# A two-block network on one NeuronCore: the SBUF tensors laid out at other start addresses

## The reference

```python
def first_block(x, ...):            # one layer
    mod = silu(c) @ ada_w + ada_b   # nine modulation vectors
    h = h + 0.5 * g1 * rmsnorm(swiglu(y, ...))        # 1024 -> 2816 -> 1024
    h = h + g2 * rmsnorm(token_mix(y, ...))           # mLSTM heads and HGRN2 heads, w_in, w_out
    h = h + 0.5 * g3 * rmsnorm(swiglu(y, ...))

def second_block(x, ...):           # two layers
    m = neighborhood_attention(...) or diff_attention(...)
    x = x + rms_norm(m, g[1])
    f = conv_glu_ffn(rms_norm(x, g[2]), ...)          # 1024 -> 2 * 2816 -> 1024
    x = x + rms_norm(f, g[3])
    x = x + sigmoid(rms_norm(x, g[4]) @ ple_w_gate) * (p @ ple_w_proj)
```

## The kernel before

| tensor | begins at | past 512 |
|---|---|---|
| h | 16512 | 128 |
| yh, yl, ph, pl | 32896, 49280, 53376, 57472 | 128 |
| raw, wh, wl | 65664, 82048, 98432 | 128 |
| acc, cst | 127232, 131328 | 256 |
| hidh, hidl | 139008, 184064 | 256 |
| oh, ol, gh, gl, moh, mol | 139008 to 188160 | 256 |
| PT, dv, qkh | 179968, 171776, 211712 | 256 |

## Time and profile before

### The profile page before, as it was taken

How to read it: one execution, slowest core, us unless ns; L and a number is a source line. 1 busy time by engine, 2 the same in 40 slices (tenths; PEclk the granted TensorE clock), 3 DMA queues, 4 the chain that set the end, 5 groups by cost and what they waited for, 6 DMA issues and landing times.

```text
span 2619.6 us, 29183 instructions
## 1 busy us (share of the span) xinstructions
PE 2494.6 (95%) x11538; PEld 1977.7 (75%) x11538; DVE 1523.7 (58%) x2379; ACT 1008.7 (39%) x1547; POOL 154.3 (6%) x166
## 2 busy tenths in 40 slices
PE   7999998989987999998999999999999999999998
PEld 4878876867766888886877688887777767888876
DVE  5876436677647333336654855534866668555445
ACT  4222234444545322223444433333545554333333
POOL 0000111000010000010101000001100010000100
PEclk9999999999999999999999999999999999999999
DMA  9555427422212333222321222222232212222321
GB/s 365 170 193 193 143 89 157 105 53 54 60 42 67 111 98 98 93 89 73 99 79 57 95 98 97 93 97 93 81 102 70 79 39 91 97 97 93 104 86 65
DMA packets 233704, 265.90 MB, mean 102 GB/s; under 512 B 8376, under 2 KB 222008, under 8 KB 233568
## 3 DMA queue, kind: packets, MB, share of 16 engines
q1 hardware_dynamic: 220704, 223.39, 28.1%
q0 software_dynamic: 11088, 37.46, 4.4%
q10 hardware_dynamic: 1776, 3.18, 0.3%
HBM read 259.78 MB, written 10.75 MB: 103 GB/s over the span
## 4 chain that ended last, share of the span: by engine, by line
PE 62%; DVE 6%; issue 3%; ACT 3%; POOL 0%; DMA 0%; POOLq 0%; ACTq 0%; DVEq 0%
PE G L2044 54%; DVE wl L1343 1%; PE X L2044 1%; PE G L2499 1%; PE X L2479 1%; ACT yh L820 1%; DVE yl L1369 1%; DVE h L1432 1%; PE G L2437 1%; DVE tmpA L1384 1%; PE X L2404 1%; PE X L2488 1%; ACT wh L771 1%; PE X L2418 0%; DVE nbias L1821 0%
## 5 line engine op out<-in xcount | busy, mean ns | idle before, releaser
L1343 DVE TENSOR_TENSOR wl<-raw,wh 128x1024 fp32r<-128x1024 f32 (+1 forms) x398 | 474.8, 1199 | 695.3 <-ACT wh L771 695.0
L2044 PE MATMUL G<-yh,wh 128*128 128x512 f32 x1864 | 754.2, 405 | 49.9 <-DVE yl L1361 15.7
L2044 PE MATMUL G<-yl,wh 128*128 128x512 f32 x1864 | 732.7, 393 | 0.0
L2044 PE MATMUL G<-yh,wl 128*128 128x512 f32 x1864 | 732.3, 393 | 0.0
L771 ACT ACTIVATE wh<-raw 128x1024 fp32r<-128x1024 f32 (+1 forms) x398 | 410.0, 1037 | 821.0 <-PE G L2044 803.0
L2044 PEld LDWEIGHTS G<-yh,wh 128*128 128x128 f32 x1864 | 353.9, 190 | 150.1 <-issue 31.5
L2044 PEld LDWEIGHTS G<-yl,wh 128*128 128x128 f32 x1864 | 353.5, 190 | 76.1
L2044 PEld LDWEIGHTS G<-yh,wl 128*128 128x128 f32 x1864 | 354.0, 190 | 71.6 <-issue 2.4
L2044 PE MATMUL G<-hidh,wh 128*128 128x512 f32 x704 | 279.7, 397 | 0.0
L2044 PE MATMUL G<-hidl,wh 128*128 128x512 f32 x704 | 278.0, 395 | 0.0
L2044 PE MATMUL G<-hidh,wl 128*128 128x512 f32 x704 | 278.0, 395 | 0.0
(11 more groups left out here) (351 smaller groups left out, 3001.3 us busy)
## 6 DMA issues: line engine op xcount, KB each, us to landing
raw<-in_ffn_w_in SPq DMA_DIRECT2D x44, 1024.0 KB, 5.0
raw<-in_ffn_w_gate SPq DMA_DIRECT2D x22, 1024.0 KB, 5.4
raw<-in_ffn_w_up SPq DMA_DIRECT2D x22, 1024.0 KB, 5.3
ada_c<-in_ada_w POOLq DMA_DIRECT2D x20, 1024.0 KB, 5.6
raw<-in_ffn_w_down SPq DMA_DIRECT2D x16, 1024.0 KB, 5.1
raw<-in_w_in SPq DMA_DIRECT2D x16, 1024.0 KB, 9.5
raw<-in_ffn_w_out SPq DMA_DIRECT2D x16, 1024.0 KB, 5.3
ada_z<-in_ada_w SPq DMA_DIRECT2D x14, 1024.0 KB, 10.9
```

The costliest lines, as they stand in the source:

```text
L1343: nc.vector.tensor_tensor(place(wl), src, f32(place(wh)), ALU.subtract).then_inc(lo, 1)
L2044: ins = nc.tensor.matmul(bank, a, b, start=first and i == 0, stop=last and i == 2)
```

## The change

It reorders the `sb(...)` calls and lays five small tensors into unused columns of others. No instruction is added, removed or moved: on every engine the instructions stand in the same order before and after, with the same shapes; only names of small tensors differ (`silc` is a part of `sm`, `t5` of `lamc`, `small` of `mod`, `rcol` of `lbc`).

```diff
+        cst = sb("cst", [P, 320])
+        sm = sb("sm", [P, 32])
         h = sb("h", [P, KT, S])
 ...
         yl = sb("yl", [P, KT, S], F32R)
+        coef = sb("coef", [P, 6, KT])
+        lbc = sb("lbc", [P, 4, NH])
         raw = sb("raw", [P, 2, UNIT])
         wh = sb("wh", [P, 4, KT, P], F32R)
         wl = sb("wl", [P, 4, KT, P], F32R)
         A2 = sb("tmpA", [P, 2, S])
+        acc = sb("acc", [P, S])
+        R = sb("rstd", [P, S])
+        ms = sb("ms", [P, S])
         with ExitStack() as c:
             ada_c = sb("ada_c", [P, UNIT], F32, c)[:, :]
+        C2 = sb("tmpC", [P, 2, S])
         B2 = sb("tmpB", [P, 2, S + 16])
-        C2 = sb("tmpC", [P, 2, S])
-        acc = sb("acc", [P, S])
-        R = sb("rstd", [P, S])
-        cst = sb("cst", [P, 320])
 ...
         ones = sb("ones", [P, P])
-        ms = sb("ms", [P, S])
         vec = sb("vec", [P, 448])
-        small = sb("small", [64, 16])
         mod = sb("mod", [P, 80])
-        coef = sb("coef", [P, 6, KT])
-        lbc = sb("lbc", [P, 4, NH])
-        sm = sb("sm", [P, 32])
+        small = mod[0:64, 72:80]
         lamc = sb("lamc", [P, 16])
-        t5 = sb("t5", [32, 16])
-        silc = sb("silc", [P, 16])
-        rcol = sb("rcol", [P, 16])
+        t5 = lamc[0:32, 8:16]
+        silc = sm[:, 24:32]
+        rcol = lbc[:, 3, :]
```

## The result

The changed kernel takes 2604.74 us (median of 4 runs, 2601.19 to 2609.38) against 2623.36 us before: a ratio of 0.9934, 95% interval 0.992 to 0.9949. It is faster by 18.6 us, clear of the scatter but under 1%, where I had forecast 91. The profiled execution is the slowest of the four, 2609.38 us, with a span of 2607.6.

What follows compares the result with a forecast made beforehand. The prediction took the distance between PE's matmul starts as the bound; gains of 38.9 + 33.6 + 18.6 = 91 us gave 2532 us, likeliest case 2485 to 2560, 8 in 10 within 2485 to 2630.

Steps and rivals of the forecast that it cites:

- What bounds the kernel: Whole kernel: it is as long as its matmuls, set by the distance between two matmul starts on PE.
- The excess depends on layout: All full-rate matmuls: the 13.3 to 20.1 ns over 213.3 depend on start addresses and need not be there.
- the feed-forwards' first half: 4224 matmuls with `yh`/`yl` moving go from 226.7 to 217.5 ns, fully on the path: 38.9 us gained.
- the second half: Feed-forwards, 2112 matmuls with `hid` moving go from 233.4 to 217.5 ns, fully on the path: 33.6 us gained.
- the rest: Stretches where PE sometimes waits, 1368 and 960 matmuls: 26.5 us, of which 0.7 counted, 18.6 us gained.
- The lower bound: New distance per matmul at best, from the plain float32 stream: 213.3 + 1.3 = 214.6 ns.
- the first rival: Only `hid`, `oh` and the like gain; all stand at 226.7 ns, a fixed price per weight load; about 2611 us, chance 0.15.
- the likeliest case: All matmuls with moving activations: the excess mostly goes, to about 217.5 ns each; 2532 us, chance 0.55.
- The rival "nothing": `yh` and `hid` differ for some reason other than addresses; the time stays at 2623 us, chance 0.12.
- The slower rival: Excess grows with the distance between moving and stationary starts: 240 ns at 256 apart, +96 us, 2719 us, chance 0.18.
- Weights as moving operand: 1152 matmuls with weights moving: taken as 0, between ends of +7.7 us and -13.8 us.
- The factor 0.7: Share of the gain outside the dense stretches that reaches the time, as PE waits there; from 0.4 to 1.

Runs made afterwards that it cites:

- two tables: Two kernels of matmuls alone, with moving or stationary tensors placed at many starts: 227.1 to 233.3 ns per matmul in one, 226.7 to 234.2 in the other.
- the finer streams: Kernel of matmuls alone, weights moved in steps from 16 bytes, then other shapes: 226.7 ns at 0 and 16 bytes apart, 233.1 at 32.

## Why the prediction was wrong, step by step

**What bounds the kernel: right.** PE's matmul starts set the time in the dense stretches, and the time followed them there in each of the layouts.

**The excess depends on layout: half right.** Between 226.7 and 233.4 ns it does. The 13.3 ns below do not. The step that failed is in the change part by part: "From above, for the case that the excess mostly goes, I take half of today's smaller one, 220 ns. I take about the middle, 217.5 ns." It rests on "neither needs to be there". Measured: 226.4 to 227.0 ns in the streams of 512 columns after, and no pair of starts in two tables under 226.7. The term for the feed-forwards' first half, 38.9 us, was therefore 0; that for the second half, 33.6 us, was 2112 x 6.7 = 14.2; of that for the rest, 18.6 us, at most 5.4 could be there. The lower bound was taken from a plain float32 stream at half the rate, and no row showed a stream at full rate near it; the lowest fp32r stream of 512 separate columns in the runs has 226.7. What I had in hand and set too low was the first rival's argument, the equal 13.3 ns with 512 and 256 columns, a fixed price that does not care for shape. The time measured lies inside my range for 8 in 10, 2485 to 2630 us, but by this rival, to which I had given 0.15, and outside the likeliest case's own range, 2485 to 2560: that is luck and not a confirmation.

**The first rival: right in its distances, wrong in its reason.** It said 226.7 for all and 2611 us; measured are about 226.5 and 2604.7, since the 4 to 8 us that it charged for the moving weights were not lost. It is not the start at 256 that was bad but the 128 bytes between it and the weights: moved to a multiple of 512 alone, `hid` kept 233.2 ns, and at 128 with the weights at 128 it had 226.9.

**The rival "nothing": refuted.** `hid` fell by 6.9 ns, and the time by 18.6 and 16.1 us in two measurements.

**The slower rival: right in its reason, wrong in its size.** The distance between the operands counts, but with a period of 256 bytes. I had two points of that curve, 0 and 128, and drew a line through them to 240 ns at 256. The layout with the weights at 128 is the slower case that can really be reached, 232.3 ns and a ratio of 1.0075.

**Weights as moving operand: the value 0 was right, by luck.** 120.0 ns before and after. I had taken 0 as lying between two ends, and neither end came. The lower one, 108 ns "if the distance between the two counts", was wrongly derived: their distance to the stationary activation was already 0 and went to 256. That 0 and 256 are the same place on the curve would explain 120.0 ns, but at 128 apart these products took 118.2, so they do not seem to follow the curve at all; why is open.

**The factor 0.7 stays open.** Of 18.6 us gained, 14.2 are `hid` in the dense stretches, which leaves 4.4 of 960 x 5.6 = 5.4 us for the rest. In the layout with the weights at 128 nearly nothing of the mixed stretches reached the time. In the traces themselves, the four stretches with `hid` moving, from their first start to their last, take 501.6 us before and 488.3 after, 13.3 less; everything else up to the end of the last matmul takes 2112.8 us before and 2114.1, 2111.6, 2111.3 and 2110.2 in the four layouts at 0 or 256 apart. So of the 5.4 us between -1.3 and 2.6 showed, which speaks for less than 0.7, but one profile of each, scattering by 4 us, can't fix the factor.

**The Trainium skill's 215.8 ns** (TensorE: Matmul & The Clock Gate, Back-to-back issue gap) agrees with the plain bf16 streams, 215.8 ns, and with no fp32r stream here. The Trainium skill, SBUF — State Buffer, section SBUF: two separate sides, says that TensorE (PE) never waits on anyone. That is about other engines, and no run here speaks against it; but the start addresses of TensorE's own two operands, moving and stationary, change the distance by up to 7.5 ns per matmul (226.7 to 234.2).

## What to carry to other kernels

For fp32r matmuls with 128 weight columns and 512 moving columns put the moving and the stationary tensor at starts that are equal modulo 256 bytes; it costs at most a filler of some bytes, and a wrong one costs 1 to 3% of each matmul (229.2 to 234.2 ns against 226.7). Before shifting a whole layout, list these differences for each pair of tensors: here only one region was off, and 128 bytes put it right. And when an excess is split into a part that varies and a part that is the same in every row, forecast only the part that varies; the constant part needs evidence of its own that something can remove it.

## What the runs showed that I had not expected

- The curve over the distance is steep at its start: 226.7 ns at 0 and 16 bytes, 233.1 at 32, 229.2 at 64 with the weights at 0 and moving at 64 but 233.1 the other way round (moving at 0, weights at 64). It is no smooth ramp and not symmetric.
- Products with the weights moving, 256 columns, lose nothing at 128 bytes apart: 118.2 ns.
- A plain bf16 stream becomes 10 ns slower per matmul by a step of two columns alone.
- With 64 moving columns an fp32r matmul took longer than with 128 or 192: 7.37 / 48 = 153.5 ns against 111.3 ns (timeline of the finer streams, starts 223.06, 228.40, 233.74 and 241.11).
